# Moving GpSimd's layer-norm weight and bias from the seam between sublayers into the next sublayer

## The reference

```python
def layer_norm(x, g, b):
    mu = jnp.mean(xf, -1, keepdims=True)
    var = jnp.mean(jnp.square(xf - mu), -1, keepdims=True)
    return ((xf - mu) * lax.rsqrt(var + LN_EPS) * g + b)

def modulated_sublayer(x, mod, g, b, fn, res_w):
    shift, scale, gate = mod[:, 0, None, :], mod[:, 1, None, :], mod[:, 2, None, :]
    y = fn(x * (1.0 + scale) + shift)
    return layer_norm(DEEPNORM_ALPHA * x + res_w * (1.0 + gate) * y, g, b)
```

## Time and profile before

| | us |
|---|---|
| median of three runs | 1284.13 |
| the profiled execution: span from first to last instruction | 1283.1 |
| TensorE busy in it | 1144.7 (89%) |
| VectorE busy | 823.9 (64%) |
| ScalarE busy | 485.9 (38%) |
| GpSimd busy | 234.8 (18%) |

### The profile page before, as it was taken

How to read it: one execution, slowest core, us unless ns; L and a number is a source line. 1 busy time by engine, 2 the same in 40 slices (tenths; PEclk the granted TensorE clock), 3 DMA queues, 4 the chain that set the end, 5 groups by cost and what they waited for, 6 DMA issues and landing times. The chain is left out here.

```text
span 1283.1 us, 14861 instructions
## 1 busy us (share of the span) xinstructions
PE 1144.7 (89%) x5205; PEld 916.4 (71%) x5205; DVE 823.9 (64%) x930; ACT 485.9 (38%) x666; POOL 234.8 (18%) x341
## 2 busy tenths in 40 slices
PE   1799999969988788999998899999889887999995
PEld 1688778747765456788787688888667676788883
DVE  6588688755565316796446799489565738444554
ACT  0543334325672103343443334343235533443440
POOL 0111221044232113210000411111143103000001
PEclk9999899879987768999999899999779998999997
DMA  8799889715451110897555399599114331665630
GB/s 317 263 318 375 299 315 357 247 31 170 132 164 52 47 33 33 312 369 275 164 191 196 125 370 356 206 364 353 41 58 148 99 99 59 204 197 197 197 98 33
DMA packets 145098, 252.28 MB, mean 197 GB/s; under 512 B 10386, under 2 KB 102802, under 8 KB 145043
## 3 DMA queue, kind: packets, MB, share of 16 engines
q1 hardware_dynamic: 124336, 176.98, 41.1%
q0 software_dynamic: 20560, 74.05, 15.4%
q10 hardware_dynamic: 146, 0.53, 0.1%
HBM read 250.48 MB, written 1.05 MB: 196 GB/s over the span
## 5 line engine op out<-in xcount | busy, mean ns | idle before, releaser
L1042 DVE TENSOR_TENSOR w_lo<-w_raw,w_hi 128x2048 fp32r<-128x2048 f32 (+2 forms) x164 | 364.5, 2226 | 150.8 <-ACT w_hi L771 150.6
L1476 PE MATMUL bank<-w_hi,hT_hi 128*128 128x512 f32 (+3 forms) x944 | 391.4, 415 | 32.6 <-DVE hT_lo L1075 25.0
L1479 PE MATMUL bank<-w_hi,hT_lo 128*128 128x512 f32 (+3 forms) x944 | 375.8, 398 | 0.0
L1480 PE MATMUL bank<-w_lo,hT_hi 128*128 128x512 f32 (+3 forms) x944 | 375.6, 398 | 0.0
L771 ACT ACTIVATE w_hi<-w_raw 128x2048 fp32r<-128x2048 f32 (+2 forms) x164 | 303.1, 1854 | 41.0 <-DMA w_raw<-in_ffn_w_up_dram 31.3
L1476 PEld LDWEIGHTS bank<-w_hi,hT_hi 128*128 128x128 f32 x944 | 187.2, 198 | 75.2 <-DVE hT_lo L1075 27.4
L1480 PEld LDWEIGHTS bank<-w_lo,hT_hi 128*128 128x128 f32 x944 | 185.9, 197 | 38.4
L1479 PEld LDWEIGHTS bank<-w_hi,hT_lo 128*128 128x128 f32 x944 | 187.2, 198 | 36.3 <-issue 2.3
L823 ACT ACTIVATE arena<-bank 128x256 f32<-128x256 f32 x88 | 33.8, 384 | 385.6 <-PE bank L1480 385.6
L1054 DVE SCALAR_TENSOR_TENSOR arena<-arena,cond 128x1024 f32<-128x1024 f32 x120 | 149.5, 1279 | 17.0 <-DMA arena<-in_ada_w_dram 16.9
L1476 PE MATMUL bank<-w_hi,fT_hi 128*128 128x512 f32 x352 | 143.1, 406 | 11.8 <-DVE fT_lo L1389 11.6
(11 more groups left out here) (204 smaller groups left out, 958.3 us busy)
## 6 DMA issues: line engine op xcount, KB each, us to landing
arena<-in_ada_w_dram POOLq DMA_DIRECT2D x128, 512.0 KB, 6.1
w_raw<-in_ffn_w_gate_dram SPq DMA_DIRECT2D x88, 512.0 KB, 4.8
w_raw<-in_ffn_w_up_dram SPq DMA_DIRECT2D x88, 512.0 KB, 5.8
w_raw<-in_ffn_w_down_dram SPq DMA_DIRECT2D x88, 512.0 KB, 4.8
w_raw<-in_hyb_w_in_dram SPq DMA_DIRECT2D x26, 512.0 KB, 4.8
arena<-in_ada_w_dram SPq DMA_DIRECT2D x16, 512.0 KB, 5.3
w_raw<-in_hyb_w_out_dram SPq DMA_DIRECT2D x8, 512.0 KB, 4.0
w_raw<-in_mla_w_out_dram SPq DMA_DIRECT2D x8, 512.0 KB, 4.0
```

The lines of the kernel that those rows point to most:

```text
L1042: nc.vector.tensor_tensor(w_lo[:, j0 % RING, 0:n], w_raw[:, j0 % RAW, 0:n], w_hi[:, j0 % RING, 0:n].bitcast(F32), ALU.subtract)\
L1476: mm = nc.tensor.matmul(dst, a_hi, b_hi, start=start, stop=False)
L1479: nc.tensor.matmul(dst, a_lo, b_hi, start=False, stop=False)
L1480: return nc.tensor.matmul(dst, a_hi, b_lo, start=False, stop=stop)
```

## The change

GpSimd's multiplication and addition leave `ln_tail` and become `scale_shift(s)`, run in sublayer s for the x that came out of s - 1. It waits until both tiles' entries into s are complete (`h_ready`). In s = 2 and s = 3 it stands behind the first 24 transfers of ada_w, in s = 5 at the sublayer's start, in the mixers ahead of everything else that GpSimd does there. `ln_tail(s)` waits for `x_ready` of the sublayer before it overwrites ln_rows. In the last sublayer VectorE makes both tiles whole inside `norm`, with two fused operations each.

```diff
@@ ln_tail
+                if s > 0:
+                    pool.wait_ge(x_ready, 2 * s)
                 for v, w in enumerate((A["ln_g"], A["ln_b"])):
                     pool.dma_start(ln_rows[:, v, :], w[l, sub:sub + 1, :].broadcast_to([P, D]))\
                         .then_inc(ln_rows_in, 16)
                 for t in range(NT):
-                    u = 2 * s + t
-                    pool.wait_ge(var_ready, u + 1)
+                    pool.wait_ge(var_ready, 2 * s + t + 1)
                     nc.gpsimd.tensor_tensor(rstd[:, :], var_eps[:, :], neg_half[:, :], ALU.pow).then_inc(rstd_ready, 1)
-                    pool.wait_ge(n_ready, u + 1)
-                    if s < last_sub:
-                        pool.wait_ge(n_tr, 2 * (u + 3))
-                    elif t == NT - 1:
-                        break
-                    pool.wait_ge(ln_rows_in, 32 * (s + 1))
+
+            def scale_shift(s):
+                pool.wait_ge(h_ready, 4 * s + 4)
+                pool.wait_ge(ln_rows_in, 32 * s)
+                for t in range(NT):
                     step(nc.gpsimd.tensor_tensor(x[:, t, :], x[:, t, :], ln_rows[:, 0, :], ALU.mult))
                     step.wait()
                     nc.gpsimd.tensor_tensor(x[:, t, :], x[:, t, :], ln_rows[:, 1, :], ALU.add).then_inc(x_ready, 1)
-                if s < last_sub:
-                    pool.wait_ge(x_ready, 2 * (s + 1))
@@ GpSimd, in an ffn
                         with pool.Fori(0, 2) as i:
                             for n in range(12):
                                 ada_piece(nxt, n, i)
+                        if s > 0 and loop == 0:
+                            scale_shift(s)
...
+                    if s == last_sub:
+                        scale_shift(s)
@@ VectorE, norm(s, t), behind var_eps
+                if s == last_sub:
+                    if t == 0:
+                        dve.wait_ge(ln_rows_in, 32 * (last_sub + 1))
+                    step(nc.vector.scalar_tensor_tensor(out=x[:, t, :], in0=x[:, t, :], scalar=mean_var[:, 0:1],
+                                                        in1=ln_rows[:, 0, :], op0=ALU.subtract, op1=ALU.mult))
+                    dve.wait_ge(rstd_ready, u + 1)
+                    step.wait()
+                    nc.vector.scalar_tensor_tensor(out=x[:, t, :], in0=x[:, t, :], scalar=rstd[:, 0:1],
+                                                   in1=ln_rows[:, 1, :], op0=ALU.mult, op1=ALU.add)\
+                        .then_inc(x_ready, 1)
+                    return
@@ VectorE, at the end
-            dve.wait_ge(n_ready, 2 * last_sub + 2)
-            dve.wait_ge(ln_rows_in, 32 * (last_sub + 1))
-            step(nc.vector.tensor_tensor(x[:, 1, :], x[:, 1, :], ln_rows[:, 0, :], ALU.mult))
-            step.wait()
-            dve.wait_ge(x_ready, 2 * last_sub + 1)
-            nc.vector.tensor_tensor(x[:, 1, :], x[:, 1, :], ln_rows[:, 1, :], ALU.add).then_inc(x_ready, 1)
```

## The result

The changed kernel takes 1307.5 us (median), the kernel before 1285.9 beside it: a ratio of 1.017, interval 1.013 to 1.021, about 21.6 us slower. Its profiled execution took 1304.81 us in itself, with a span of 1303.2 against 1283.1. The forecast was 1299.8. The runs of one kernel lie up to 20 us apart, and the longer ones have the lower mean clock (the kernel after: span 1299.5 at 0.933, 1312.2 at 0.918). Part 1 of the page hardly shows the loss: TensorE, VectorE and ScalarE are as busy as before. GpSimd's busy time is up by 14.4 us for no more work: its instructions on x, 20 now and 22 before, take 64.8 us in sum instead of 55.2.

What follows compares the result with a forecast made beforehand. TensorE, busy 89% of the span, was taken as the bound, so time counts where it stands still. Terms: -8.8 - 2.6 + 12.4 + 5.8 + 6.9 + 2 = +15.7 us, giving 1299.8; range 1282 to 1309.

Steps and rivals of the forecast that it cites:

- the four places forecast: Chunk 4 of s = 2 and of s = 3, start of hyb, start of mla: 12.4, 5.8 and 6.9 us lost.
- the clock's term: TensorE's clock: 2 us lost; three new pauses in both chunks and hyb cost 5, shorter pauses at five seams save 3.
- Chunk 4, 2 x 6.2 us: In s = 2 and s = 3, GpSimd's four instructions alternate with VectorE's full queue; TensorE stands 6.2 us each, 12.4 lost.
- Start of hyb, 5.8: Start of hyb: GpSimd's four instructions delay masks and distance table, so TensorE's transposes wait for ScalarE; 5.8 us lost.
- Start of mla, 6.9: Start of mla: VectorE gets the frequencies 6.8 us later, so TensorE's transposes start late; 6.9 us lost.
- Seams, -8.8: Five seams between sublayers: without GpSimd's pair, VectorE releases TensorE's products earlier; 8.8 us gained.
- I take 0, the row's value: Seams: the accumulator's clearing, now beside tile 1's normalisation, was assumed to cost nothing, as against a split.
- rival 3: Seams into s = 2 and s = 3: the accumulator's clearing delays tile 1's normalisation, gain shrinks by 2.5 us, 1302.3; 15%.
- End, -2.6: Kernel's end: residual without GpSimd beside it gains 1.9 us, fused operations behind the variance 0.7; 2.6 gained.
- rival 1: Chunk 4: GpSimd's instructions find pauses, taking away 12.4 us and 3 of the clock, 1284; 10%.
- rival 2: Chunks, hyb and mla all hide the work; only seams, end and their clock stay: -14.4 us, 1269.7; 12%.
- rival 4: Clock at its worst: each new pause costs 3 us, seams save nothing, +9 in place of +2, 1306.8; 8%.

Runs made afterwards that it cites:

- The run with the steps first: Changed kernel, but in s = 2 and s = 3 GpSimd's weight and bias of x also wait for the 24th modulation step: 1290.4 us, ratio 1.002.
- the one without the work: Changed kernel without GpSimd's multiplications and additions on x, only the signal given, in all sublayers but the last: 1275.7 us, ratio 0.992.
- the one with memsets: Changed kernel, six write-only memsets of x replacing GpSimd's four instructions in ffn sublayers, hyb and mla without weight and bias: 1274.9 us, ratio 0.992.
- the best combination: Changed kernel, weight and bias behind the 24th modulation step in s = 2, 3, at the seams into hyb, mla; accumulator cleared after both entries: 1273.7 us, ratio 0.991.

## Why the prediction was right, and where it was off

- *Which way, and by what.* Right: the loss stands in the four places forecast, half of it in the two chunks, though hyb (8.8) lost more than mla (6.9). The run with the steps first and the one without the work show it from both sides. The amount owes something to luck. The trace has +20.1 us where the sum said 15.7. Behind the chunks' waits 9.6 us were lost, where the clock's term had 5 for them and hyb together, and two seams came out 6.1 worse. Against that, 5.1 were gained where nothing had changed, and the seams into the mixers gave 5.1 more than forecast.
- *Chunk 4, 2 x 6.2 us.* The mechanism was right to the order of instructions. The take_lo was forecast to end at 601.0 less the shift, which was 0.8 here; it ended at 599.38. The pauses were 5.10 and 4.49, a little under, since each hand-over between the two engines came some 0.1 us sooner than the added durations say. GpSimd's first instruction is recorded from 582.61, beside the split before it; its end, 585.87, is the forecast's 586.8 less the shift.
- *Clock, +2 us.* **This is the mis-sized term.** I gave three new pauses 1.7 to 3 us each and added them up to 5 in all, which is their lower end. Behind the wait, chunk 4 lost another 4.3 and 5.3 us (9.6 and 10.0 less the step of the waiting product itself, 5.3 and 4.7) and hyb 1.9. How much of the chunks' part is the pause's stays open: without a pause there the same stretches lose 3.3 and 3.3 us in the run without the work, 0.0 and 3.2 in the one with memsets, and 1.6 and 0.0 both with the steps first and with only the end changed.
- *Start of hyb, 5.8.* The wait was 6.9 by the matmuls' starts, with the releaser forecast. Of the 1.1 above the forecast 0.7 is the distance table's first line, 2.13 us where it was 1.42 (L658 now, L655 before); the other 1.9 of the stretch's 8.8 is clock.
- *Start of mla, 6.9.* Exact by size. Its reason was half the truth: the frequencies were late, but the run with them first shows VectorE held by GpSimd's instructions all the same, for all but 1.8 us.
- *Seams, -8.8.* Each seam's first product came 0.82 us earlier, as forecast; with the clock's part the seams into the mixers gave more than forecast (3.8 for 3.1 into hyb, some 3 for 1.9 into mla). The step that failed is "I take 0, the row's value" for the clearing: the row was that of a split, and L1128 is another form. It cost +1.0 and +2.1 where -1.1 and -1.9 were due, 6.1 us apart with the clock's part in it, and more than rival 3's 2.5. That 2.5 was itself too small: by the prediction's own figures a normalisation 2.6 us late ends 0.3 later than before, so that it takes the whole 1.1 and 1.9 of these seams and 0.3 at each besides, 3.6 in all. The rest is in the new wait at s = 3, 3.67 us, and the half-clock products behind it. The Trainium skill's page "SBUF — State Buffer", Who interferes with whom, had it right where I chose against it: by that rule, a `tensor_scalar` in its fast mode is held by a GpSimd instruction that only writes, and a VectorE instruction with two on-chip inputs is not. The trace agrees with both halves: 3.12 for 0.81 us on L1143, and 2.28 and 2.47 beside 11.20 us of memsets.
- *End, -2.6.* Found -1.5 behind the start of the last product. I had set 1.7 us of tile 0's fused operation inside a pause of 1.6. The power of tile 0 took 1.53 us, not 0.55, beside the first fused operation, so the residual of tile 1 started 1.4 us behind the end of TensorE's last product.
- *Rivals.* 1 and 2 were wrong as forecasts, but rival 2's 1269.7 is close to what can be had in other places: 1273.7 in the best combination. Rival 3's collision happened. The measured 1307.5 lies nearest rival 4's 1306.8, but that rival is right in part only: the new pauses did cost more, while the seams into the mixers gained by the clock.
- *Range.* Its lower end of 1282 is not the sum that its words say: rival 1's 1284 with the seams at 15.5 instead of 8.8 would be 1277.7.
